# Two kinds of waits in a one-core decoder step: where conv's next weights are split in ScalarE's queue, and which output blocks an FFN input product waits for

## The reference

```python
def short_conv_mixer(h, prev, w_in, conv_k, w_out):
    b, c, u = jnp.split(h @ w_in, 3, axis=-1)
    cu = c * u
    buf = jnp.concatenate([prev, cu], axis=1)
    y = conv_k[0] * buf[:, 0:T]
    for j in range(1, CONV_WIDTH):
        y = y + conv_k[j] * buf[:, j:j + T]
    return (b * y) @ w_out, buf[:, -(CONV_WIDTH - 1):]

def swiglu(x, w_in, w_out):
    g, u = jnp.split(x @ w_in, 2, axis=-1)
    return (jax.nn.silu(g) * u) @ w_out

# each layer:  x += mixer(rmsnorm(x));  x += swiglu(rmsnorm(x));  at the end one more rmsnorm
```

## Time and profile before

| | us |
|---|---|
| median of 3 runs | 2998.09 (2991.74 to 3000.66) |
| the profiled execution, whole | 2997.41 |
| its span, first to last instruction | 2995.6 |
| TensorE busy with matmuls | 2637.7 |
| VectorE busy | 1672.3 |
| GpSimd busy | 1549.8 |
| ScalarE busy | 975.4 |

### The profile page before, as it was taken

One profiled execution on the slowest core, in us unless ns is written; L12 is line 12 of the kernel. 1 busy time (PEld: TensorE's weight loads), 2 busy tenths in 40 slices (PEclk: granted clock), 3 DMA queues, 4 the chain that ended last, 5 costly groups with the idle time before them and its releaser, 6 DMA issues. The chain is left out here.

```text
span 2995.6 us, 45376 instructions
## 1 busy us (share of the span) xinstructions
PE 2637.7 (88%) x18580; PEld 2392.6 (80%) x18580; DVE 1672.3 (56%) x1857; ACT 975.4 (33%) x1811; POOL 1549.8 (52%) x880
## 2 busy tenths in 40 slices
PE   6989999998697999999999677686979999999996
PEld 4666666665597999999999577686969999999996
DVE  5656666665457665566656331212385666556664
ACT  4456666566533222222222301000242222222223
POOL 2766665664047656665664401111377655666553
PEclk9999999998898999999999888888989999999998
DMA  8667776775611112111111001010112111111111
GB/s 279 221 225 240 261 263 228 241 252 192 228 43 43 50 43 57 43 50 43 50 50 43 22 28 43 21 42 15 46 39 57 46 47 43 57 43 50 43 50 58
DMA packets 240172, 291.81 MB, mean 97 GB/s; under 512 B 12851, under 2 KB 193172, under 8 KB 239846
## 3 DMA queue, kind: packets, MB, share of 16 engines
q1 hardware_dynamic: 217410, 271.17, 28.2%
q10 hardware_dynamic: 22420, 16.82, 1.7%
q0 software_dynamic: 144, 1.05, 0.1%
HBM read 267.76 MB, written 21.28 MB: 96 GB/s over the span
## 5 line engine op out<-in xcount | busy, mean ns | idle before, releaser
L754 POOL TENSOR_TENSOR w_lo<-raw,w_hi 128x1024 fp32r<-128x1024 f32 (+1 forms) x100 | 249.0, 2494 | 879.7 <-ACT w_hi L993 517.1
L1931 PE MATMUL PS<-a_all,wb 128*128 128x258 f32 x3520 | 584.5, 286 | 90.3 <-DVE x_res L2449 56.7
L1931 PEld LDWEIGHTS PS<-a_all,wb 128*128 128x128 f32 x3520 | 494.2, 192 | 102.6 <-issue 69.1
L2449 DVE TENSOR_TENSOR x_res<-PS,x_res 128x1032 f32<-128x1032 f32 x360 | 443.6, 1232 | 212.7 <-PE PS L1943 111.5
L1943 PE MATMUL PS<-wb,w_hi 128*128 128x344 f32 x2112 | 407.1, 328 | 19.0 <-POOL w_lo L754 10.5
L781 POOL TENSOR_TENSOR kpage<-kpage,q_bc 128x1024 f32<-128x1024 f32 x128 | 304.9, 2399 | 127.1 <-DMA kpage<-in_cache_k 94.7
L1943 PEld LDWEIGHTS PS<-wb,w_hi 128*128 128x128 f32 x2112 | 333.7, 189 | 46.0 <-DVE x_res L2449 31.1
L1931 PE MATMUL PS<-c_lo,wb 128*128 128x258 f32 x1760 | 356.8, 284 | 0.0
L1514 PE MATMUL PS<-a_all,w_hi 128*128 128x344 f32 x1152 | 226.8, 335 | 103.0 <-POOL w_lo L754 102.6
L1514 PEld LDWEIGHTS PS<-a_all,w_hi 128*128 128x128 f32 x1152 | 200.1, 200 | 105.3 <-POOL w_lo L754 66.2
L1931 PEld LDWEIGHTS PS<-c_lo,wb 128*128 128x128 f32 x1760 | 275.1, 191 | 0.0
(11 more groups left out here) (306 smaller groups left out, 5286.2 us busy)
## 6 DMA issues: line engine op xcount, KB each, us to landing
kpage<-in_cache_k SPq DMA_DIRECT2D x128, 512.0 KB, 4.7
vpage<-in_cache_v SPq DMA_DIRECT2D x128, 512.0 KB, 5.1
raw<-in_w_ffn_in SPq DMA_DIRECT2D x88, 512.0 KB, 4.6
raw<-in_w_ffn_out SPq DMA_DIRECT2D x44, 512.0 KB, 3.5
raw<-in_attn_w_qkvf SPq DMA_DIRECT2D x24, 512.0 KB, 5.0
vpage<-in_attn_w_qkvf SPq DMA_DIRECT2D x24, 512.0 KB, 5.0
raw<-in_conv_w_in SPq DMA_DIRECT2D x24, 512.0 KB, 3.8
out<-raw ACTq DMA_DIRECT2D x16, 512.0 KB, 7.8
```

What stands on the lines that cost most here:

```text
L754: gp.tensor_tensor(w_lo[s][:, 0:kts, 0:cols], raw[s][:, 0:kts, 0:cols], w_hi[s][:, 0:kts, 0:cols].bitcast(F32), ALU.subtract).then_inc(w_l ...
L1931: ins = pe.matmul(out[:, b, :], w[:, k, :], h[:, x, k, b * (HN // 2):(b + 1) * (HN // 2)], start=k == 0 and n == 0, stop=k == HK - 1 and n ...
L2449: dve.tensor_tensor(blocks(x_res[:, m, :]), group(s), blocks(x_res[:, m, :]), ALU.add).then_inc(ev[s], 1)
```

## The change

In ScalarE's conv loop the range of splits is moved by two, so that for tile f the splits of products 3f+2, 3f+3 and 3f+4 stand ahead of the wait for `prd`, where 3f, 3f+1 and 3f+2 stood. In `in_pair` the wait for both halves of the output adds ahead of c = 0 is divided: c = 0 waits for `ev[0]` (even blocks), c = 1 for `ev[1]` (odd blocks).

```diff
             for f in range(KT):
-                for r in range(max(2, 3 * f), 3 * f + 3):
+                for r in range(max(2, 3 * f + 2), min(3 * KT, 3 * f + 5)):
                     high(r % 2)
                 act.wait_ge(prd, pr.up())
                 act.activation(bt(f)[0], t3[:, :], ACT.Copy).then_inc(bhi, 1)
...
                     pe.wait_ge(wls, 7 * jj + at[c])
                     if c == 0:
                         pe.wait_ge(iv, 8 * jj)
-                        for s in range(2):
-                            pe.wait_ge(ev[s], evd[s].value + 1)
+                    if c < 2:
+                        pe.wait_ge(ev[c], evd[c].value + 1)
                     if c == 2 and j == 0:
```

## The result

The changed kernel takes 2838.61 us in the median of four runs (2831.34 to 2841.16), the kernel before 2996.89 us in the same comparison. The ratio is 0.947 with an interval of 0.945 to 0.949. The forecast was 2836 us. The profiled execution took 2841.16 us, 2839.3 us of it span.

What follows compares the result with a forecast made beforehand. TensorE, 88% busy, was taken as the bound, held up by waits in conv and FFN. 2997.4 - 104.8 (conv) + 0.2 (jumps) - 56.7 (FFN) = 2836.1, carried as 2836 us; range 2827 to 2866 us.

Steps and rivals of the forecast that it cites:

- two waits named: TensorE's leading waits: conv's product helper for GpSimd's low parts, 128.4 us; FFN input products for VectorE's adds, 56.7 us.
- conv chain: Conv tile end: VectorE's inside, ScalarE's copy, only then two splits and GpSimd's low parts; TensorE idle 12.61 us.
- conv term: Conv stage: seven tiles go from 48.94 to 33.96 us each, a gain of 104.8 us, at least 88 us.
- stretched inside: VectorE's work at a conv tile's end grows by up to 2.1 us beside GpSimd's low part, at no cost.
- jump back: TensorE's conv loop, tiles 4 and 6: two jumps lie open; rival that they stall, up to 25 us, chance 0.05.
- near end: Low estimate for conv's two loop jumps: 0.2 us for both, from 0.08 us seen; the other end 12.6 us each.
- FFN term: FFN pair steps: the first input product starts 1.42 us earlier in 40 handovers, a gain of 56.7 us.
- lower bound of 48 us: FFN handovers: 1.2 us won each if the release lag doubles or weights load less smoothly.

Runs made afterwards that it cites:

- run moved by one: Changed kernel with conv's splits moved by one product in place of two (3f+1 to 3f+3 ahead of tile f's inside): 2849.57 us, ratio 0.951.
- run moved by three: Changed kernel with conv's splits moved by three products (3f+3 to 3f+5 all ahead of tile f's inside): 2835.54 us, ratio 0.9455.
- written-out loop: Changed kernel with TensorE's conv loop of three passes written out, so no jump back is left: 2842.05 us in a single run.

## Why the prediction was right

**What bounds, and the chain.** The two waits named were the two that went. The conv chain was read rightly: the run moved by one shows that what matters is where the splits stand in ScalarE's queue and nothing in the inside itself, since the inside is as long there as it was before, 7.8 us from the third read to the copy.

**The size of the conv term.** 103.85 us against 104.8. The tile takes 34.10 us where the working had 33.96. The step that was off, by 0.4%, is the pace: the mean of two intervals, 11.28 and 11.36 us, was taken, but the first follows a slow product and is short in VectorE's reads alone. TensorE's own product starts there, 1766.07 and 1777.44, lie 11.37 us apart. In the changed kernel the second and third reads of every tile lie 11.36 or 11.37 us apart, and three of those are the tile. That TensorE would never be late, and that the granted clock would stay at 1.00 once the gap is gone, held.

**The stretched inside.** The working allowed 2.1 us and a read one microsecond late; the trace has 2.2 us and 1.1 us. The cover was thinner than it looked at one point. ScalarE's spare time ahead of the split of 3f+5 was put at 2.4 us without the stretch, and 0.34 us of it are left. No run uses it up. By the trace there was more cover behind it: the low part that follows this split ends at 1732.12 and TensorE starts the product that needs it at 1739.70, 7.6 us later. The run moved by three shows the other half, that VectorE's read may come 4.7 us late at no cost.

**The jump back.** The near end, 0.2 us for both, was taken, and the rows on instruction packets were the reason. The 0.08 us that it rests on were no mark of a jump: in the run moved by one the waits ahead of tiles 4 and 6, where the jumps lie, are 1.22 us, and those ahead of tiles 3, 5 and 7, where none lies, are 1.28 to 1.29 us. The written-out loop shows the cost to be nothing that a tile time in hundredths of a microsecond can tell. The rule of the Trainium skill (Runtime: NRT & Kernel Launch, section Instruction fetch mechanics) on taken branches to pages that are not held did not come to bear, as no packet came in the later passes.

**The FFN term.** 57.0 us alone by medians, against 56.7; the 1.43 us by which a step is shorter make 57.2 us in 40 steps. The gap did close whole, as the working said. L2516 did move behind L923, as the working said, and cost TensorE nothing. The lower bound of 48 us, kept for a handover that loads weights less smoothly, was not needed.

**The sum and the range.** The touched stretches sum to 161.7 us against 161.3 in one trace and to 157.8 in the other, so the agreement to 0.4 us is luck: the conv term came out 0.95 us under the working and the FFN stretches of that trace 1.1 us over it. By medians the change is worth 158.3 us. The distance from 2836 to the median of 2838.6 is within the spread of the runs, 10 us for the changed kernel.

## What to carry to other kernels

Look in an in-order queue for work that needs nothing from the instruction it stands behind. Here two splits behind a copy cost 15 us a tile, 12.6 us of it idleness and the rest a slow start behind it, with the granted clock at 0.50 at first. Count how far to move it by what must be ready within the covering product: one place too few cost 1.5 us a tile, one place too many nothing. And where one wait stands for two buffers, ask which of them the next instruction writes.

## What the runs showed of the hardware that was not expected

Where VectorE's two-input multiply met a GpSimd subtraction in these traces, the one that started second waited for the first to finish, and the wait is inside its duration. GpSimd's low part began at 1718.36 and ended at 1720.75; VectorE's multiply began at 1718.43 and took 3.41 us, so it ended at 1721.84, 1.09 us after GpSimd did, though it takes 1.23 us alone. In one tile of the changed kernel the order is the other way round:

```profile
1854.83 1.23 DVE L2571 TENSOR_TENSOR c_f<-c_f 128x1032 f32<-128x1032 f32 x1
1856.10 2.25 DVE L2572 COPY conv_rows<-c_f 128x10 f32<-128x10 f32 x1
...
1855.06 3.26 POOL L754 TENSOR_TENSOR w_lo<-raw,w_hi 128x1024 fp32r<-128x1024 f32 x1 [9.27 <-ACT w_hi L993]
```

There VectorE's multiply began first and kept its 1.23 us, and GpSimd's subtraction took 3.26 us in place of 2.39. The small copy behind the multiply took 2.25 us in place of 0.17 and ended with GpSimd's subtraction. The Trainium skill says as much of the two operations (SBUF — State Buffer, section Who interferes with whom): a VectorE instruction with two SBUF inputs and a GpSimd instruction that reads SBUF exclude each other for the whole of the one that issued first. This trace agrees, with 3.41 us for 1.23 on VectorE and 3.26 us for 2.39 on GpSimd. So a longer row in a trace need not mean more work.

A wait of 1.2 us between conv products cost about 0.25 us more than itself and left the granted clock at 1.00. A wait of 12.6 us cost 2.3 us more than itself (14.8 us a tile in all), with the clock at 0.50 when the matmuls came back. The FFN waits of 1.42 us cost 1.43 us a step, so hardly more than themselves.
